# Four moves in the order of an attention stage: key turning, V weighing, row maxima, rotation

## The reference, cut to what matters

```python
n = rms_norm(h, norm1_g); p = n @ w_in            # -> qA kA vA qB kB vB
qa = rope(rms_norm(qa, qn_g)) * scale             # 8 query heads, 2 key heads of 64
ka = rope(rms_norm(ka, kn_g))
oa = softmax(qa @ ka.T) @ va                      # A: all 256 keys
ob = softmax_with_sink(qb @ kb.T + bias) @ vb     # B: |i - j| <= 128
mix = concat([rms_norm(oa, gnorm_a), rms_norm(ob, gnorm_b)])
h = h + mix @ w_o
h = h + hier_moe(rms_norm(h, norm2_g), ...)       # top group of 4, top 2 of its 8 experts
out = rms_norm(h, final_g)                        # 32 experts, each 3 x 2 MB of weights
```

## Time and profile before

| what | us |
|---|---|
| median of 3 runs | 591.22 (590.34 to 592.71) |
| the profiled execution | 591.22 |
| its span in the profile | 589.4 |
| TensorE busy | 438.9 (74%) |
| VectorE busy | 116.3 (20%) |
| ScalarE busy | 63.9 (11%) |
| GpSimd busy | 28.2 (5%) |

### The profile page before, as it was taken

The page is one execution under the profiler, slowest core; times in us unless marked ns, Lnnn a source line. Parts: engine busy times, 40 slices in busy tenths (PEclk is TensorE's granted clock), DMA queues, the critical chain, the costliest instruction groups (busy, mean ns, idle before and its releaser), DMA issues.

```text
span 589.4 us, 6189 instructions
## 1 busy us (share of the span) xinstructions
PE 438.9 (74%) x2545; PEld 203.1 (34%) x2545; DVE 116.3 (20%) x283; ACT 63.9 (11%) x128; POOL 28.2 (5%) x58
## 2 busy tenths in 40 slices
PE   3999989968999999999453856475638453756394
PEld 2445757546444343535111411141114111411031
DVE  1005666243202020203000300030003000300023
ACT  2013333131010000010000000000000000000002
POOL 2032020040000000000000000000000000000001
PEclk9999999987999999999876976698769976976598
DMA  6899591741899999999999999999999999999981
GB/s 246 344 401 431 230 409 20 300 173 46 301 359 429 421 431 425 427 426 427 427 433 425 428 426 430 425 430 426 428 429 426 428 429 427 425 431 427 409 341 73
DMA packets 24094, 217.67 MB, mean 369 GB/s; under 512 B 5056, under 2 KB 6360, under 8 KB 12544
## 3 DMA queue, kind: packets, MB, share of 16 engines
q1 hardware_dynamic: 19824, 214.31, 87.2%
q10 hardware_dynamic: 4240, 2.94, 1.6%
HBM read 216.18 MB, written 1.06 MB: 369 GB/s over the span
## 4 chain that ended last, share of the span: by engine, by line
PE 57%; DMA 37%; DVE 2%; issue 1%; POOL 1%; SPq 0%; ACT 0%; ACTq 0%; DVEq 0%; POOLq 0%
PE bank L1215 20%; DMA ring<-in_w_up_dram 16%; DMA ring<-in_w_down_dram 10%; PE bank L1230 10%; DMA ring<-in_w_gate_dram 10%; PE bank L1012 7%; PE bank L1081 4%; PE bank L1187 4%; PE bank L1250 4%; PE bank L1071 2%; PE bank L995 2%; PE bank L1060 1%; PE bank L1049 1%; DMA region_t<-in_norm_g_dram 1%; PE bank L1154 1%
## 5 line engine op out<-in xcount | busy, mean ns | idle before, releaser
L1215 PE MATMUL bank<-ring,region_x 128*32 128x512 f32 (+1 forms) x1024 | 160.9, 680 | 110.1 <-DMA ring<-in_w_gate_dram 57.4
L1215 PEld LDWEIGHTS bank<-ring,region_x 128*32 128x32 f32 (+1 forms) x1024 | 47.2, 130 | 221.6 <-issue 221.6
L1230 PE MATMUL bank<-ring,region_q 128*32 128x512 f32 (+1 forms) x512 | 75.9, 638 | 12.6 <-DMA ring<-in_w_down_dram 11.4
L885 DVE TENSOR_TENSOR region_q<-region_q,bank 128x512 f32<-128x512 f32 x10 | 6.9, 689 | 331.9 <-PE bank L1215 331.9
L1230 PEld LDWEIGHTS bank<-ring,region_q 128*32 128x32 f32 (+1 forms) x512 | 23.7, 122 | 57.8 <-issue 56.1
L1012 PE MATMUL bank<-ring,region_x 128*128 128x512 f32 x96 | 42.3, 595 | 0.8 <-DVE region_x L656 0.8
L1187 PE MATMUL bank<-region_q,region_t 128*128 128x128 f32 x320 | 39.5, 284 | 1.8 <-DVE region_q L872 1.8
L1250 PE MATMUL bank<-region_x,region_q 128*128 128x512 f32 x80 | 38.9, 618 | 0.7 <-ACT region_x L617 0.7
L1187 PEld LDWEIGHTS bank<-region_q,region_t 128*128 128x128 f32 x320 | 38.7, 201 | 1.8 <-issue 1.8
L891 DVE TENSOR_TENSOR h<-h,bank 128x512 f32<-128x512 f32 x40 | 27.5, 687 | 18.5 <-PE bank L1250 18.5
L1081 PE MATMUL bank<-ring,region_q 128*128 128x512 f32 x64 | 28.9, 597 | 0.0
(11 more groups left out here) (179 smaller groups left out, 238.6 us busy)
## 6 DMA issues: line engine op xcount, KB each, us to landing
ring<-in_w_up_dram SPq DMA_DIRECT2D x32, 2048.0 KB, 31.4
ring<-in_w_gate_dram SPq DMA_DIRECT2D x31, 2048.0 KB, 29.4
ring<-in_w_down_dram SPq DMA_DIRECT2D x27, 2048.0 KB, 31.1
ring<-in_w_down_dram SPq DMA_DIRECT2D x20, 512.0 KB, 12.9
ring<-in_w_in_dram SPq DMA_DIRECT2D x8, 768.0 KB, 9.3
ring<-in_w_o_dram SPq DMA_DIRECT2D x2, 2048.0 KB, 11.4
ring<-in_w_gate_dram SPq DMA_DIRECT2D x4, 512.0 KB, 6.8
ring<-bias_line ACTq DMA_DIRECT2D x1, 1536.0 KB, 15.0
```

The costliest lines, as they stand in the source:

```text
L885: dve.tensor_tensor(act_sb, silu_sb, ps[UP][:], ALU.mult).then_inc(act_done, 1)
L1215: last = pe.matmul(ps[bank][rows, :], xgT[:, c, rows], slots[fill_slot(f + a)][:, c * F:(c + 1) * F], start=(c == 0), stop=(c == KC - 1))
L1230: last = pe.matmul(ps[GD0 + half][rows, :], hT[:, c, rows], slots[fill_slot(f + a)][:, c * D + 512 * half:c * D + 512 * half + 512], start ...
```

## The change

Only the order of calls changes; every operation is still there, with the same shapes and data.

- TensorE, ahead of the loop: the second half of `global_q(0)` comes before the turning of A's keys.
- TensorE, step 2: `weigh_v(1)` comes before the turning of tile 0's A queries. `turn_mix(1, 0, 7)` goes to the end of step 2, behind `scores(4)`, from step 3.
- VectorE: `maxima(3)` goes from step 2 to the head of step 3.
- VectorE, step 3: `rotate(1)` comes before `mix_out(1, 0, 1)`.

```diff
--- before.py
+++ after.py
@@ -747,15 +747,13 @@
                 dve.tensor_tensor(qt_, qt_, bcast(rq[t], 2, HD), ALU.mult).then_inc(roped, 1)
 
             for s in range(8):
-                if s != 3:
-                    maxima(s)
+                maxima(s)
                 if s >= 1:
                     cut_probs(s - 1)
                 if s == 0:
                     dve.wait_ge(qk_turned, 4)
                     dve.tensor_copy(qkT[:, 4, :], ps[5][:, 256:512]).then_inc(qkT_ready, 1)
                 if s == 2:
-                    maxima(3)
                     dve.wait_ge(qkv_done, 4)
                 if s >= 2:
                     outputs(s - 2)
@@ -764,8 +762,8 @@
                 if s == 2:
                     turn_out(5, 0)
                 if s == 3:
+                    rotate(1)
                     mix_out(1, 0, 1)
-                    rotate(1)
                 if s == 4:
                     dve.wait_ge(ro_ready, 1)
                     add_projection(1, 0, 0, 1, 7)
@@ -1091,21 +1089,18 @@
             scores(0)
             scores(1)
             turn(ps[6], [pair_cols(1, b) for b in range(5, 9)], qk_turned)
+            global_q(0, range(4, 8))
             pe.wait_ge(k_roped, 1)
             turn(ps[5][:, 256:512], [pair_cols(t, 4) for t in range(TT)], qk_turned)
-            global_q(0, range(4, 8))
             pe.wait_ge(qkT_ready, 4)
             for s in range(8):
                 turn_probs(s)
+                if s >= 1:
+                    weigh_v(s - 1)
                 if s == 2:
                     pe.wait_ge(roped, 1)
                     pe.wait_ge(qkv_cut, 6)
                     turn(ps[7], [pair_cols(0, b) for b in range(0, 4)], qk_turned)
-                if s == 3:
-                    turn_mix(1, 0, 7)
-                if s >= 1:
-                    weigh_v(s - 1)
-                if s == 2:
                     pe.wait_ge(qkT_ready, 5)
                 if s == 4:
                     pe.wait_ge(roped, 2)
@@ -1120,6 +1115,8 @@
                     global_q(1, range(0, 4))
                 if s == 1:
                     global_q(1, range(4, 8))
+                if s == 2:
+                    turn_mix(1, 0, 7)
                 if s == 3:
                     pe.wait_ge(mixT_ready, 1)
                     pe.wait_ge(w_o_in[1], 16)
```

## The result

The changed kernel takes 599.31 us (median of 12 runs, 593.76 to 601.55), the kernel before 591.91 (12 runs, 589.64 to 593.20). The record holds 17 more executions of the changed kernel; the median of all 29 is 597.78. The ratio of the means, over all of them, is 1.0108 with a 95% interval of 1.0081 to 1.0135: 6.4 us slower, 4.8 to 8.0. The prediction had 593.9 and a range of 591.0 to 596.5. It had the sign and missed the size. The scatter has grown too, from 3.6 us between the lowest and the highest of 12 runs to 7.8.

A forecast was written before the change was run, and what follows sets the result against it. The prediction took TensorE's list to bound the attention and weight bandwidth the late experts. It added 0.77 (keys) and 1.88 (from `global_q(1)`'s end to `turn_probs(4)`), 2.65 in all, to 591.22: 593.9 us, range 591.0 to 596.5.

The forecast's parts named there:

- Keys late, +0.77: Ahead of TensorE's loop: the copy of A's turned keys is waited for in the open, 0.50, plus 0.27 refill.
- `weigh_v(1)` ahead, +0.95: TensorE, step 2: the copy out of bank 7 is no longer hidden, so `scores(4)` ends 0.95 us later.
- The stall ahead of `turn_mix(1, 0)`, 2.2 us: End of step 2: TensorE waits 2.2 us for `outputs(1)`, which stands on VectorE behind the copy, `maxima(3)` and `cut_probs(2)`.
- The tie ahead of `project`: Step 3: `mix_out` lets `project` start at +11.74, TensorE is free at +11.71; cost 0 to 0.1 us.
- the wait of 1.06 gone: Ahead of `turn_probs(4)`: TensorE's former 1.06 us wait for step 4's exponentials disappears.
- A delay of the attention reaches the end one to one: Attention to kernel end: routed loads and TensorE both start from what TensorE has finished, so a delay arrives in full.
- the second rival: Routing: arriving 2.65 us later, TensorE may keep its clock there, saving 3.6 us; 590.3 us, chance 0.06.
- So I keep the full clock for the sum, with little to spare: Stall ahead of `turn_mix(1, 0)`: clock assumed to stay at 1.00 (2.4 GHz), as during 2.12 us of idle at 524.68.
- the first rival: New stall ahead of `turn_mix(1, 0)`: the clock falls and costs 2.2 us more; 596.1 us, chance 0.13.
- The row that I leaned on: Profile row at 524.68 us: 2.12 us of TensorE idle, read as having passed at clock 1.00.
- The rule of the Trainium skill on transposes: Behind the new stall: transposes do not count as busy like matmuls, making the quiet stretch 3.7 us, so the clock falls.
- G: End of `global_q(1)` on TensorE, from which later times are counted: 66.67 us before, forecast 67.44 with the change.

## Why the prediction was wrong

- *Keys late, +0.77*: the stall came as worked out (0.52 idle plus the restart, 0.74 in all), the cover of `maxima(1)` and its exponentials held. Right in the trace; too small for the time of a whole run to prove.
- *`weigh_v(1)` ahead, +0.95*: 0.21 and 0.78 us of idle, `scores(4)` ends at +5.41 where +5.25 was forecast. Right within 0.2 us.
- *The stall ahead of `turn_mix(1, 0)`, 2.2 us*: 2.15. Right in size and cause, and the one move behind it, `maxima(3)`, is what the loss hangs on: put back, 593.55. Alone it costs 3.4 us of the 6.4; alone, the keys and `weigh_v(1)` show 0.4 and 0.5, neither clear of zero.
- *The tie ahead of `project`* and *the wait of 1.06 gone*: right. In the changed kernel TensorE was slow there and proves nothing; the run with transposes in the stall shows it at full clock, with `project` at 79.21 and `turn_probs(4)` at 82.75, and no wait ahead of either. At full clock the whole sum of 2.65 was measured as 2.2, 1.3 to 3.2.
- *A delay of the attention reaches the end one to one*: nearly. 9.13 us at the router's last matmul were 8.44 at the first routed load and 7.9 at the end. The 1.2 given back are in part the routing's clock, so the second rival came true in a small part; in the second trace of the changed kernel the routing's low stretch was 17.1 us, longer than before, so this is luck of the execution.
- *"So I keep the full clock for the sum, with little to spare"*: this is the step that failed, with the first rival's two numbers. I gave the fall a chance of 0.13; both traces of the changed kernel show it, and of its 32 executions only five (593.76 to 595.35) lie below 596 us. I gave it 2.2 us, priced by one gather; it cost 5.0, since 10.1 us ran at half pace. The bound of 3.0, from the longest low stretch I quoted, was no bound: in the routing of the same trace the clock stayed low for 13.7 us.
- The row that I leaned on was misread. The 2.12 us of idle at 524.68 were no wait that passed at full clock. They are the first part of a wait of 10.70 us, cut off where the clock fell; the row shows a fall after 2.12 us of idle, and so spoke for the rival. In the changed kernel, too, the stall was at 1.00 and the fall came 0.6 us behind it. The kernel before, the stretch behind the row's end and the matmuls that ended the wait:

```profile
526.80:527.40 0.60, 0.00 (x0) 0.00 (x0) 0.00 (x0) 0.00 (x0) 0.00 (x0) 0.50 0.96 410
```

```profile
535.33 9.59 PE L1215 MATMUL bank<-ring,region_x 128*32 128x512 f32 x64 [10.70 <-DMA ring<-in_w_gate_dram]
```

- The rule of the Trainium skill on transposes (TensorE: Matmul & The Clock Gate, Part 4: PE-mode transpose) pointed to the right rival for a reason that two traces here contradict: 20 transposes in the stall kept the clock at 1.00, 32 behind it brought it back.

## What to carry to other kernels

Where TensorE is the bound, a new stall is priced twice: its own length, and what runs behind it at half pace if the clock falls, which can be more than the stall itself. How long it stays low could not be told beforehand: the same kinds of mixed work ran 3.4 us at the lower level in one kernel and 10.2 in another. When you read a stretch of idle time off a trace as harmless, read on to its end and a few microseconds beyond. And before moving code to remove such a stall, fill it: unused matmuls or transposes into a free bank, no longer than the wait, kept the clock up in the traces, won back some 4 us here (594.22 against the changed kernel's 598), and in the routing 2.7 us.

## What the runs showed that I had not expected

- A stall of 1.54 us brought the clock down from 2.4 to 1.2 GHz in the attention, while waits of 1.05, 0.91 and 0.78 us passed at 1.00 in every trace that has them.
- After the fall it came back after 3.4 us, with wide matmuls, with transposes and with mixed work in one kernel, and after 10.2 us of mixed work in two traces of another.
- The low stretch of the routing, where nothing had been changed, lasted 10.2, 13.7 or 17.1 us, the first and the last in two executions of one and the same kernel.
- Twenty transposes in a row held the clock at 1.00, in the one trace of it, in a stretch that otherwise lost it.
- The first 64 projection matmuls took 27.73 us in six traces and 29.38 to 30.16 in the other eight, whatever the kernel. With the 0.74 of the keys, where they are late, this is nearly all of the spread of G (66.5 to 70.1 us).
